# A hybrid decoder step: the S5 near table multiplied once per tile and part, its repetitions written by 16 copies

## What is computed

```python
ab = exp(dt * a)                      # complex, per group and state
x[t] = ab * x[t-1] + g * (B @ u[t])   # B: 64 states x 16 channels
y[t] = Re(C @ x[t]) + d * u[t]        # C: 16 channels x 64 states
```

## Time and profile before

| what | us |
| --- | --- |
| median of 3 runs | 750.63 |
| lowest and highest run | 750.08, 754.21 |
| span of the profiled execution | 751.2 |
| TensorE busy in it | 713.0 (95%) |
| VectorE busy | 541.9 (72%) |
| ScalarE busy | 407.2 (54%) |
| mean granted clock of TensorE | 0.984 of full speed |

### The profile page before, as it was taken

How to read it: one execution, slowest core, us unless ns; L and a number is a source line. 1 busy time by engine, 2 the same in 40 slices (tenths; PEclk the granted TensorE clock), 3 DMA queues, 4 the chain that set the end, 5 groups by cost and what they waited for, 6 DMA issues and landing times.

```text
span 751.2 us, 17486 instructions
## 1 busy us (share of the span) xinstructions
PE 713.0 (95%) x7214; PEld 657.8 (88%) x7214; DVE 541.9 (72%) x967; ACT 407.2 (54%) x769; POOL 43.5 (6%) x58
## 2 busy tenths in 40 slices
PE   5999879999999999999989899999999999999994
PEld 4877757869999999999979797877989999999993
DVE  7996885277787988874775987556878877555474
ACT  4514043365687566773558424365558764677342
POOL 5000021200000000000030001010000000000001
PEclk9999988999999999999999999999999999999998
DMA  8531214346465565555524212331635555655531
GB/s 335 203 126 38 88 58 140 130 151 211 124 201 181 169 195 173 190 175 166 173 82 141 81 64 86 131 140 66 205 130 200 172 184 178 183 183 181 185 113 58
DMA packets 30718, 112.50 MB, mean 150 GB/s; under 512 B 3536, under 2 KB 3744, under 8 KB 30256
## 3 DMA queue, kind: packets, MB, share of 16 engines
q1 hardware_dynamic: 28080, 100.78, 41.6%
q0 software_dynamic: 1984, 9.54, 3.3%
q10 hardware_dynamic: 576, 1.08, 0.4%
HBM read 107.20 MB, written 4.18 MB: 148 GB/s over the span
## 4 chain that ended last, share of the span: by engine, by line
PE 75%; DVE 8%; ACT 3%; issue 1%; DVEq 0%; ACTq 0%
PE stream L1081 21%; PE stream L1082 20%; PE stream L1083 20%; PE stream L1056 5%; DVE w_low L1611 1%; PE mix L983 1%; PE mix L788 1%; PE mix L861 1%; PE mix L821 1%; PE mix L883 1%; PE mix L833 0%; PE mix L970 0%; DVE scratch L1943 0%; DVE scratch L2184 0%; PE mix L711 0%
## 5 line engine op out<-in xcount | busy, mean ns | idle before, releaser
L1611 DVE TENSOR_TENSOR w_low<-w_raw,w_high 128x1024 fp32r<-128x1024 f32 x161 | 197.0, 1223 | 107.2 <-ACT w_high L1140 105.0
L1140 ACT ACTIVATE w_high<-w_raw 128x1024 fp32r<-128x1024 f32 x161 | 170.4, 1058 | 149.3 <-PE stream L1083 134.8
L1081 PE MATMUL stream<-a_high,w_high 128*128 128x264 f32 x520 | 154.7, 298 | 2.7 <-DVE a_low L2198 2.7
L1082 PE MATMUL stream<-a_low,w_high 128*128 128x264 f32 x520 | 148.6, 286 | 0.0
L1083 PE MATMUL stream<-a_high,w_low 128*128 128x264 f32 x520 | 148.3, 285 | 0.0
L1081 PE MATMUL stream<-h_high,w_high 128*128 128x264 f32 x512 | 146.3, 286 | 0.0
L1083 PE MATMUL stream<-h_high,w_low 128*128 128x264 f32 x512 | 145.1, 283 | 0.0
L1082 PE MATMUL stream<-h_low,w_high 128*128 128x264 f32 x512 | 145.0, 283 | 0.0
L1056 PE MATMUL stream<-X,w_raw 128*128 128x264 f32 x400 | 99.2, 405 | 9.1 <-DMA w_raw<-in_weights 7.9
L1081 PEld LDWEIGHTS stream<-a_high,w_high 128*128 128x128 f32 x520 | 99.0, 190 | 7.3 <-issue 5.4
L1056 PEld LDWEIGHTS stream<-X,w_raw 128*128 128x128 f32 x400 | 77.7, 199 | 26.6 <-DMA w_raw<-in_weights 8.3
(11 more groups left out here) (389 smaller groups left out, 989.6 us busy)
## 6 DMA issues: line engine op xcount, KB each, us to landing
w_raw<-in_weights SPq DMA_DIRECT2D x190, 512.0 KB, 3.6
mats<-in_matrices POOLq DMA_DIRECT2D x2, 1024.0 KB, 5.9
S_hg<-in_state_hg POOLq DMA_DIRECT2D x2, 768.0 KB, 7.6
out_hg_s<-S_hg POOLq DMA_DIRECT2D x2, 768.0 KB, 3.7
consts<-in_constants POOLq DMA_DIRECT2D x1, 1499.5 KB, 10.0
X<-in_xT ACTq DMA_DIRECT2D x4, 264.0 KB, 4.9
out_y<-X SPq DMA_DIRECT2D x4, 264.0 KB, 2.1
S_rt<-in_state_rt POOLq DMA_DIRECT2D x2, 512.0 KB, 8.6
```

Of the source, the lines that this page charges most:

```text
L1081: pe.matmul(bnk[:, 0:width], wh, xh, start=(first and kk == 0), stop=False)
L1082: pe.matmul(bnk[:, 0:width], wh, xl, start=False, stop=False)
L1140: act.activation(w_high[:, SPLIT_SLOT[n], :], w_raw[:, RAW_SLOT[n], :], ACT.Copy).then_inc(high_ready, 1)
L1611: put(tt(w_low[:, SPLIT_SLOT[n], :], w_raw[:, RAW_SLOT[n], :], w_high[:, SPLIT_SLOT[n], :].bitcast(F32), ALU.subtract), low_ready)
```

## The change

The near table is multiplied by one unit instead of two. For each tile and each of the two parts r (real and imaginary) there is one matmul of 128 columns, that of distances 0 to 3; four tiles jj lie on the four column groups, and the two groups of four tiles (h) side by side in one bank. ScalarE writes the shifted repetitions into `s5_near` with 16 copies, four per row block i (`near_copies`): the copy (i, jj) reads partitions 32jj of the bank and writes partitions 32i, with columns 0 to 127-32i of two tiles. In layer 0 all 16 follow each other where the 8 stood. For layer 1 the four of row block i = c-1 stand at the end of ScalarE's steps c = 1 to 4, and both former places (in `norm(0)` and at c == 5) are empty.

```diff
@@ TensorE
             def s5_tab_near(l, u):
-                lx, h = u[1:]
+                lx = u[1]
                 pe.wait_ge(pow_ready, 2 * lx + 1)
                 b = unit(l, u)
-                for jj in range(4):
-                    j = 4 * h + jj
+                for h in range(2):
                     for r in range(2):
-                        for i in range(S5_STEP):
-                            o = b[32 * i:32 * i + 32, 128 * jj + 32 * i:128 * jj + 128]
-                            mm = pe.matmul(o, BT_s5[:, r, j, :], tab_out[:, r, j, 0:S5_STEP - i, :].rearrange("p d c -> p (d c)"),
-                                           start=(r == 0), stop=(r == 1), tile_position=(0, 32 * i))
+                        for jj in range(4):
+                            j = 4 * h + jj
+                            o = b[32 * jj:32 * jj + 32, 128 * h:128 * h + 128]
+                            mm = pe.matmul(o, BT_s5[:, r, j, :], tab_out[:, r, j, 0:S5_STEP, :].rearrange("p d c -> p (d c)"),
+                                           start=(r == 0), stop=(r == 1), tile_position=(0, 32 * jj))
                 mm.then_inc(unit_done, 1)
@@ ScalarE
+            def near_copies(l, lx, i):
+                b, fu = got(l, ("s5_tab_near", lx))
+                bv = b[:, 0:256].rearrange("p (h n) -> p h n", h=2)
+                for jj in range(4):
+                    act.activation(s5_near[32 * i:32 * i + 32, jj:S5_TILES:4, 32 * i:128], bv[32 * jj:32 * jj + 32, :, 0:128 - 32 * i],
+                                   ACT.Copy).then_inc(tab_ready, 1)
+                if i == S5_STEP - 1:
+                    copied(tab_ready, TAB_COPIES * (lx + 1), fu)
@@ ScalarE, layer 0
                 if l == 0 and c == 12:
                     act.wait_ge(cleared, 1)
-                    table_copies(0, 0, 1)
-                    table_copies(0, 0, 2)
+                    for i in range(S5_STEP):
+                        near_copies(0, 0, i)
@@ ScalarE, norm
-                if l + 1 < DEPTH:
-                    table_copies(l, l + 1, 1)
@@ ScalarE, steps of layer 1
                             ln2_output(l - 1, 2 * c - 2)
                             ln2_output(l - 1, 2 * c - 1)
+                            near_copies(l - 1, l, c - 1)
-                    if l and c == 5:
-                        table_copies(l - 1, l, 2)
```

More of the change, by code:

```diff
@@ L109 @@
 _plan(10, ("s5_sel",), layers=(0,))
-_plan(11, ("hg_level", 1, 0), ("hg_level", 1, 1), ("s5_in", 0), ("s5_tab_near", 0, 0), ("s5_tab_near", 0, 1), layers=(0,))
+_plan(11, ("hg_level", 1, 0), ("hg_level", 1, 1), ("s5_in", 0), ("s5_tab_near", 0), layers=(0,))
 _plan(12, ("hg_level", 2, 0), ("hg_level", 2, 1), ("s5_in", 1), layers=(0,))
@@ L156 @@
     _plan(TABLES_AT, *[("s5_tab_in", _l + 1, _t) for _t in range(4)], layers=(_l,))
-    _plan(N_CHUNKS - 1, *[("s5_tab_near", _l + 1, _h) for _h in range(2)], layers=(_l,))
+    _plan(N_CHUNKS - 1, ("s5_tab_near", _l + 1), layers=(_l,))
 STOPS = ({19: (3, 6), 21: (4,), 22: (2, 5, 6, 7), UP_A + 1: (3, 5)}, {17: (3, 6), 21: (4,), 22: (2, 4, 6), UP_A + 1: (3, 5)})
@@ L195 @@
 PACKED_LEVELS = 5
+TAB_COPIES = 4 + 4 * S5_STEP
 def build(nc, xT, weights, vectors, matrices, constants, level_masks, state_hg, state_rt, state_s5,
@@ L659, in s5_in @@
                     pe.wait_ge(ustep_ready, l + 1)
-                    pe.wait_ge(tab_ready, 12 * l + 4)
+                    pe.wait_ge(tab_ready, TAB_COPIES * l + 4)
                 b = unit(l, u)
@@ L680, in s5_out @@
                 if u[1] == 0:
-                    pe.wait_ge(tab_ready, 12 * (l + 1))
+                    pe.wait_ge(tab_ready, TAB_COPIES * (l + 1))
                     need(pe, y5_free, l)
@@ L1153, in s5_rot, with table_copies @@
                 act.activation(rot[:, :, :, :], turns[l][:, 0:1024].rearrange("p (r j k) -> p r j k", r=2, j=S5_TILES), ACT.Sin).then_inc(rot_ready, 1)
[L1155 to L1169, removed]
+            def table_copies(l, lx):
+                for t in range(4):
+                    b, fu = got(l, ("s5_tab_in", lx, t))
+                    act.activation(tab_in[:, 2 * t:2 * t + 2, :, :], b[:, :].rearrange("p (j r n) -> p j r n", j=2, r=2), ACT.Copy).then_inc(tab_ready, 1)
+                    copied(tab_ready, TAB_COPIES * lx + t + 1, fu)
+            def near_copies(l, lx, i):
[6 more added lines that the diff above has]
+                    copied(tab_ready, TAB_COPIES * (lx + 1), fu)
             def near_top(l, r):
@@ L1255, in mixer_work @@
                 if l == 0 and c == 11:
-                    table_copies(0, 0, 0)
+                    table_copies(0, 0)
                 if l == 0 and c == 12:
                     act.wait_ge(cleared, 1)
-                    table_copies(0, 0, 1)
-                    table_copies(0, 0, 2)
+                    for i in range(S5_STEP):
+                        near_copies(0, 0, i)
                 if c == S5_FROM[l] + 1:
@@ L1560, in _ @@
                     if c == TABLES_AT + 1 and l + 1 < DEPTH:
-                        table_copies(l, l + 1, 0)
-                    if l and c == 5:
-                        table_copies(l - 1, l, 2)
+                        table_copies(l, l + 1)
                 norm(l)
```

## The result

The changed kernel takes 760.12 us (759.19 to 765.52, 4 runs) and the kernel before 752.42 us (750.08 to 755.74, 4 runs, with those of the table above): a ratio of 1.0095, 95% interval [1.0058, 1.0132]. The forecast was 756.3 us, range 751.5 to 758.5. The direction is as forecast, the time lies above the range.

A forecast was written before the change was run, and what follows sets the result against it. The prediction took ScalarE to set the pace: its copies before step 12 in layer 0 and its early work in layer 1. Terms 0.5 + 2.0 + 0 + 3.2 = +5.7 us on 750.63 gave 756.3 us, range 751.5 to 758.5.

The forecast's parts named there:

- the last of the sum: Whole kernel: span 751.2 becomes 756.9; that execution lies 0.57 above the median 750.63, so the median becomes 756.3.
- Matmuls, 1.1 us a unit: Near table on TensorE: the new unit's 32 records take 1.1 us, where 128 took 3.68.
- Start of the copies 0.86 us sooner: Layer 0: fewer matmuls let ScalarE start copying 0.4 to 0.9 us earlier, taken as 0.86.
- Copies don't overlap, 5.0 us: ScalarE: 16 copies with changing source partitions lie 0.02 us apart and take 5.0 us; overlapped, 3.2.
- Rival B: ScalarE copies in both layers overlap like L1331 and L1332; 751.0 to 752.0 us, chance 0.12.
- Step 12 starts 0.5 us later: Layer 0: `tr_hk_sample` waits for the last of 16 copies, so dense step 12 starts 0.5 us later.
- The clock, +2.0 us (0 to 2.6): Layer 0: some 4.5 us of TensorE idling lowers its clock at about 71 us, lengthening step 12 by 2.0.
- Rival A: Layer 0: the idle stretch doesn't lower TensorE's clock; 754.3 us, chance 0.16.
- End of layer 0, 0 (at most 1): End of layer 0: TensorE idles about 5.2 us instead of 2.66, at no cost, at most 1 us.
- Layer 1, +3.2 us: Layer 1, steps 1 to 3: 4.1 us of copies, 0.9 absorbed by waits, delay block 6's `w_high` by 3.2.
- Rival C: Start of layer 1: TensorE, not ScalarE, sets the pace, so inserted copies are free; 751.1 to 753.1 us, chance 0.16.
- D, the matmuls' time comes through: Both table places: the matmuls' saving of 2.6 us per layer shows in the time; 745.4 us, chance 0.04.

The follow-up runs named there:

- e4: The changed kernel, but each copy reads the same partitions it writes (other table values, same amount of work): 755.58 us, ratio 1.0029.
- e12: The changed kernel once more, nothing altered, in the last round of runs: 759.23 us, ratio 1.0081 to the kernel before.
- e5: The changed kernel once more, nothing altered, in a middle round of runs: 759.42 us, ratio 1.0079 to the kernel before.
- e3: The changed kernel plus nine matmuls with unread results, filling TensorE's idle time before the waiting transpose in layer 0: 758.19 us, ratio 1.0062.
- e2: The changed kernel with layer 1's 16 copies back in the old places (`norm(0)` and c == 5): 757.57 us, ratio 1.0070.
- e10: The changed kernel with both the nine unread matmuls in layer 0 and layer 1's copies in the old places: 754.91 us, ratio 1.0019.
- e9: The changed kernel with layer 0 wholly as before and layer 1's 16 copies in the old places: 753.23 us, ratio 1.0012.
- e6: The changed kernel with layer 0's near unit last in step 11, copied after the transposed values, and layer 1's copies in old places: 752.09 us, ratio 0.9975.
- e7: The kernel before, with both layer 0 near units last in step 11 and their copies behind the transposed values: 752.23 us, ratio 0.9980.
- e1: The changed kernel with layer 0 as before (two near units, 8 copies), layer 1 as changed: 758.51 us, ratio 1.0071.
- e11: The changed kernel with layer 0's near unit last in step 11, layer 1's copies where the change puts them: 755.48 us, ratio 1.0044.

## Why the time came out above the range

**The step that failed is the last of the sum**: "The span of 751.2 becomes 756.9; that execution lies 0.57 above the median 750.63, so the median becomes 756.3." The base under it, 750.63, is the median of three runs, and those three happened to be low. The same kernel takes 752.42 with the fourth run, and 752.77, 753.42 and 752.51 over 25, 23 and 28 later ones. That is 1.8 to 2.8 us, and neither the range nor the chances had a term for it.

The sign of it was hidden by a second error, the span taken as the execution's time. Every run since shows the time 1.7 to 1.9 us above the span, two of them 2.9 (a run of before with a span of 751.2 took 752.97). So the execution whose rows made up the sum took about 753.0 us; it lay some 2.3 us above the median of three and not 0.57. This error alone doesn't move the forecast, because 751.2 is put in and taken out again: 756.3 is 750.63 + 5.7.

With the later medians, +5.7 us is 758.2 to 759.1, against a measured 759.2 to 760.1. Of the 3.8 us between 756.3 and 760.12, 1.8 is the base, and 2.0 is a difference of 7.7 us instead of 5.7, which isn't told apart from 5.7: by its interval the difference is 4.4 to 9.9 us.

- *Matmuls, 1.1 us a unit*: 1.08 us. As the prediction took it, the 128 columns paced each four before; paced by the mean of 80, the new unit would have taken 1.6 us.
- *Start of the copies 0.86 us sooner*: the bank was full at 65.6, copies from 65.76; against step 11, 0.87 sooner. Right.
- *Copies don't overlap, 5.0 us*: 5.09. The Trainium skill (ScalarE: Activation LUTs, section "What ACT_TABLE_LOAD costs") has back-to-back instructions overlapping by about 93 ns. The trace agrees with this where the next instruction stays on the same partitions (e4, 3.51 us for 16) and disagrees where it moves to others (5.09 us). The overlap in e4 is 0.09 us, the figure of the page. Rival B falls with the changed kernel and holds in e4.
- *Step 12 starts 0.5 us later*: 0.8 in the profile after against step 11's end; 0.52 of that is the late transpose (71.03 against 70.24, less 0.27), the rest the three transposes at the lower clock. Right.
- *The clock, +2.0 us (0 to 2.6)*: it fell, as forecast, and cost 1.7 us in the first and the e12 profile and 3.0 in e5's (step 12 and the transposes). e3 shows that the idle stretch is the cause. Rival A falls. The term was right, its upper bound too low by 0.4. Behind 2.70 us of idling (e4) it cost nothing.
- *End of layer 0, 0 (at most 1)*: nothing in the first and the e12 profile, 0.9 us in e5's, inside the bound.
- *Layer 1, +3.2 us*: 3.1 to 3.2 for `w_high`, `w_low` and `s5_half` 0 (in e5 3.1 from the end of step 3 on), and step 7 ends 3.16 later in the first and the e12 profile, 3.9 in e5's. e2 takes it all away. Rival C falls: the slack was the two waits of 0.37 and 0.52 us, and no more.
- *Missing from the sum, TensorE's clock in layer 1*: the prediction priced the wait for `U_step` as a delay of 2.0 us of TensorE that is hidden later. In the first and the e12 profile it is (step 4 ends 1.9 us late). In e5's the clock falls behind this wait of 1.8 us, and step 4 ends 4.9 late.
- *Missing from the sum, step 8 of layer 1*: from 1.6 us gained (e5) over 0.8 lost (first profile) to 2.2 us lost (e12). What is lost lies in a wait of TensorE of 0.7 to 0.8 us on no visible releaser (L705) and, in e12, a longer stretch at the lower clock; e5's granted clock stays at 1.00 from 438 to 446, where before has 0.58 at 430 to 434. e2's profile loses 2.2 without the copies, e10's 0.9, e9's nothing. So it isn't firmly tied to the copies; what decides it stays open.
- *D, the matmuls' time comes through*: not in this change; in e6, where the copies no longer stand between, 2.6 us of it do in layer 0's profile.

So +5.7 was measured as +6.0 to +7.7 (759.42 - 753.42, 759.23 - 752.51, 760.12 - 752.42), and each of the three intervals holds 5.7. From the end of step 11 of layer 0 to the end of step 11 of layer 1, the three profiles lose 5.9 (first, without the 6.4), 5.1 (e5) and 7.6 us (e12). The mechanisms were the right ones, and in the two places what they cost varies by 2 us and more with the clock. The base was about 2 us low.

The range stood on that base too. The bounds of the terms in it add up to +4.7 to +8.2 us, which is 755.3 to 758.8 on 750.63 (the prediction says 754.5 to 758.5) and 757.1 to 760.6 on 752.42, with the measured time inside.

## What to carry to other kernels

Fewer matmuls are worth nothing where the chain waits for what reads their result: here a saving of 2.6 us on TensorE was paid for with 1.4 us more of ScalarE in the one place where TensorE waits for it, and with 4.1 us in the one stretch where ScalarE has under 1 us of slack. First put the reader off the path (the unit last, its copies behind those that others wait for): with the copies of layer 1 in their old places that turned +0.8% into -0.25%. The same order with the old, dearer matmuls gives -0.20% (e7), so a cheaper unit wasn't shown to be worth anything in time.

Price the idle time that a change opens on TensorE, not only the delay: 4.3 us of idling cost 1.4 to 2.7 us more in the dense step behind it. The price isn't one number. It was nothing behind 2.70 us in layer 0 of e4. In layer 1 of e5 it was 3 us in the step behind a wait of 1.8 us, and 0.7 of them were left by step 7.

And give the base of a sum a range of its own. Three runs of one kernel had a median 2 us below that of 25, a third of the whole effect, and a span isn't a time: here it lay 1.7 to 1.9 us below it.

## What the hardware showed that was not expected

- ScalarE's copies, one behind the other, overlap by 0.09 us when source and destination start where those of the one before did, and lie 0.02 us apart when either moves: 3.51 against 5.09 us for the same 16. In the changed kernel the source alone moves within a row block. That the destination alone is enough shows in layer 1, behind an instruction of `ln2_output` on all partitions: the first copy of row block 0 (from partition 0 to partition 0) starts 0.09 us before its end, that of row block 1 (from 0 to 32) 0.02 us after it.
- Low-clock stretches come at places that no change touches, in some executions of a kernel and not in others: 6.4 us in steps 19 and 20 in two profiles (the changed kernel's first and e2's) of fourteen. A profile must be cleared of them before its steps are compared.
- The same wait is followed by a lower clock in one execution and not in another. Behind the 1.8 to 1.9 us for `U_step` the granted clock fell to 0.50 within 2 us in e1, e3 and e5, and stayed at 1.00 for at least 6 us in the changed kernel's first profile, in e11 and in e12. The first profile, e5 and e12 are of one and the same kernel.
- TensorE has waits of 0.3 to 2.7 us for which the profile shows no releaser. The longest in every profile stands at one place, the unit `s5_out` of layer 0 (L692 in before, 1.7 us at 93), and takes 1.0 to 2.7 us. Others come and go, even between profiles of one kernel: 0.8 us at L676 in the changed kernel's first profile and in e12, nothing there in e5; 2.1 us within a dense step of e3. They add up to 2 to 5 us a profile; what moves them was not tried.
